# Three matmul split kernel: activation tensors of five stages begin at other addresses modulo 512 bytes

## The chip, the cores and the metric

One core of a Trainium2 chip runs the program. The metric is the device time of one execution in microseconds (us), taken from several runs. The core has TensorE (PE, matmuls; its weight loads are listed as PEld), VectorE (DVE), ScalarE (ACT), GpSimd (POOL) and a queue engine (SP) that issues the weight transfers. On-chip memory (SBUF) has 128 partitions; an address here is a byte offset within a partition, the same in all 128.

## The reference

Two blocks in a row over 256 tokens of width 1024, in float32. The first: nine modulation vectors from a condition, a gated feed-forward part (width 2816) over latent and context tokens, a mixed layer (short convolution branch, grouped attention with 8 query and 2 key heads, gates, output projection), and a second feed-forward part over latent tokens. The second: an even layer (four mLSTM heads and eight stick-breaking attention heads, one output projection of 2048 rows) and an odd layer (multi-scale pooling with a small mixing matrix for each of four groups, gates, an output projection of 2048 rows). Cut to the matmuls that matter here:

```python
x = x + 0.5 * ml[2] * swiglu(modulate(rms_norm(x, norm1_g), ...), ffn1_w_in, ffn1_w_out)   # latent, and the same for the context
x = x + ml[5] * ((g_conv * (y_conv @ w_bc) + g_attn * (o_attn @ w_ba)) @ w_out)
x = x + 0.5 * ml[8] * swiglu(modulate(rms_norm(x, norm3_g), ...), ffn2_w_in, ffn2_w_out)
x = rms_norm(x, final_g)
x = x + rmsnorm(concat(ya, yb) @ w_out_ab, post_g)                 # even layer
mixed = einsum('bsgc,gce->bsge', pooled, pool_w) * pool_scale       # odd layer
x = x + rmsnorm((mixed * silu(z)) @ w_out_c, post_g)
```

## The kernel before, in words

**How a product is made.** Activations lie transposed, features on partitions and tokens along the row (T = 256 latent tokens; 512 with the context). Every weight matrix is cut into chunks of up to 4 x 128 rows by 256 columns, each one DMA into the ring `W`. ScalarE rounds a chunk into `WH` (float32r), VectorE writes the rest `W - WH` into `WL`, both rings of five slots. Activations are split in the same way into a high and a low tensor. A product is then three matmuls into one PSUM tile for each k-tile of 128 rows and each 128 output columns (lines 1048 to 1050, with the weights stationary and the activations moving), or lines 1054 to 1056 with the activations stationary and the weights moving (for `v`, `ev`, `sv` and `p1`):

```python
pe.matmul(o, h[:, k, c], xh[:, kk, a:b], start=kk == 0, stop=False)
pe.matmul(o, h[:, k, c], xl[:, kk, a:b], start=False, stop=False)
mm = pe.matmul(o, l[:, k, c], xh[:, kk, a:b], start=False, stop=kk == gm.nk - 1)
```

A matmul here has 128 stationary columns (512 bytes of a partition) and 256 or 512 moving columns (1024 or 2048 bytes). While one streams, the weight load of the next is under way.

**What sets the order.** The class `Plan` writes one list of steps before anything is built; each engine's program walks that list and does its own share, with semaphores between. Products ("gemms") are called in the order of the model, and small work (attention, mLSTM, stick-breaking, norms) is laid between their chunks. Nothing in `Plan` depends on addresses.

**Where tensors lie.** `sbuf(...)` takes the next free bytes. The rings and shared tensors come first and stay. Below them each stage has a region of its own in a `with ExitStack()` block, and the blocks reuse the same bytes; a `PAD` tensor, which nothing reads or writes, sets where a block's tensors begin. Every slot, chunk, k-tile and 128-column step is a multiple of 512 bytes, so an operand's address modulo 512 is that of its tensor. The built program has these, modulo 512:

| tensor | moving or stationary in | matmuls | address mod 512 | distance from WH, WL |
|---|---|---|---|---|
| WH, WL | all | | 320 | |
| X1H, X1L | fa1, fb1 (first feed-forward, 512 columns) | | 320 | 0 |
| GH1, GL1 | fx1 (512 columns; its last two tiles in halves of 256) | | 320 | 0 |
| XH, XL (parts of XHB, XLB) | all products of normed x, 256 columns; `k` with 512 | | 0 | 192 |
| YH, YL | mc, res | 384 | 0 | 192 |
| OH, OL | ma | 192 | 0 | 192 |
| GH2, GL2 | fx2 (second feed-forward, out) | 528 | 0 | 192 |
| ZH, ZL | p0 (even layer, out) | 384 | 0 | 192 |
| RH, RL | p1 (odd layer, out; stationary) | 384 | 0 | 192 |
| PH, PL | om (odd layer, mixing) | 192 | 0 | 192 |

"Distance" is (tensor - weights) modulo 512. Where the activations are stationary, moving minus stationary is the other way round, 320 for 192.

The stages in order of time: first feed-forward to 405 us, q, k, v and the attention beside cg, vc, bg to 550, gt and mc (YH) in turn to 612, ga, ma (OH) to 658, res (YH) to 681, second feed-forward with fx2 (GH2) twice to 875, even layer to 1121, p0 (ZH) to 1171, odd layer with om (PH) from 1221 to 1292, and p1 (RH) to 1336.

Of the kernel before, what the change touches and what calls it, by code (L numbers as in the profile page):

```python
# [844 lines left out]
def build_program(nc, w, out):  # L845
    with ExitStack() as ctx:
# [12 lines left out]
        def sbuf(st, name, shape, dt=F32):  # L859
            return st.enter_context(nc.sbuf_tensor(name, shape, dt))  # L860
# [31 lines left out]
            AC1 = sbuf(st, "AC1", [128, 4, 256])  # L892
            JK = sbuf(st, "JK", [128, 4, 256])
        with ExitStack() as st:
            sbuf(st, "PAD3", [128, 64])
            YH, YL = sbuf(st, "YH", [128, 8, T], F32R), sbuf(st, "YL", [128, 8, T], F32R)
            OH, OL = sbuf(st, "OH", [128, 8, T], F32R), sbuf(st, "OL", [128, 8, T], F32R)
            Q = sbuf(st, "Q", [128, 8, T])
            K = sbuf(st, "K", [128, 2, 512])
            VV = sbuf(st, "VV", [128, 4, T])  # L900
            MC = sbuf(st, "MC", [128, 8, T])
            U = sbuf(st, "U", [128, 2, T + 2])
            PT = sbuf(st, "PT", [128, 2, 4, T])
            SM = sbuf(st, "SM", [128, 4, 4])
        HOT = MC[:, 0, 0:131]
        with ExitStack() as st:
            sbuf(st, "PAD5", [128, 64])
            GH[2], GL[2] = sbuf(st, "GH2", [128, 12, T], F32R), sbuf(st, "GL2", [128, 12, T], F32R)
        with ExitStack() as st:
            sbuf(st, "PAD6", [128, 64])  # L910
            ZH, ZL = sbuf(st, "ZH", [128, 16, T], F32R), sbuf(st, "ZL", [128, 16, T], F32R)
            G = sbuf(st, "G", [128, 6, T])
            AT = sbuf(st, "AT", [128, 2, 4])
            CV = sbuf(st, "CV", [128, 4, T + 3])
            E = {n: sbuf(st, f"E{n}", [128, 2, 2, T]) for n in "qkvoz"}
            EW = sbuf(st, "EW", [128, 2, 384])
        with ExitStack() as st:
            sbuf(st, "PAD7", [128, 64])
            RH, RL = sbuf(st, "RH", [128, 16, T], F32R), sbuf(st, "RL", [128, 16, T], F32R)
            PH, PL = sbuf(st, "PH", [128, 2, 4, T], F32R), sbuf(st, "PL", [128, 2, 4, T], F32R)  # L920
            OZ = sbuf(st, "OZ", [128, 2, 4, T])
            PV = sbuf(st, "PV", [128, 6, 16 + T])
# [1378 lines left out]
```

## Time and profile before

| | |
|---|---|
| median of 3 runs | 1337.68 us |
| lowest, highest | 1337.42, 1344.29 us |
| profiled execution: span from first to last instruction | 1343.2 us |
| profiled execution: its own time outside the span | not given by the page |
| TensorE busy | 1312.1 us, 9320 matmul records |
| VectorE, ScalarE, GpSimd busy | 903.8, 645.0, 27.3 us |
| read from HBM | 227.63 MB, 170 GB/s over the span |

The profile lists each instruction with its start and a duration; for matmuls the ends are modelled and they overlap, so a matmul's duration (276 to 284 ns at 256 columns) is more than twice the time from one start to the next. That time between starts is what adds up to the span. "Idle before" is an engine's idle time ahead of a group and what ended it. A busy share of TensorE close to 1 means that it never ran dry, not that its matmuls followed at the highest rate.

### The profile page before, as it was taken

The page shows a single profiled execution, that of the slowest core. Times are in us where ns is not written, and L with a number is a line of the kernel's source. Part 1 is how long each engine was busy: PE and PEld are TensorE (multiplying, and loading weights), DVE is VectorE, ACT ScalarE, POOL GpSimd, SP SyncE. Part 2 cuts the span into 40 slices and gives each one's busy share as a digit, 9 for nine tenths or more (in the row PEclk, how much of TensorE's full clock was granted, in tenths as well). Part 3 has the DMA queues.
Part 4 walks back from the last instruction along what each step waited for, and adds up shares of the span by engine and source line. Part 5 has one row for each costly group of instructions (what it writes and reads, how often), then busy time and mean ns, then how long its engine had stood idle before and what let it go on. Part 6 is the DMA issues. An engine that isn't in the chain of part 4 may idle for free. (4 is left out here: it accounts for less than half of the span.)

```text
span 1343.2 us, 23450 instructions
## 1 busy us (share of the span) xinstructions
PE 1312.1 (98%) x9320; PEld 1214.2 (90%) x9320; DVE 903.8 (67%) x1461; ACT 645.0 (48%) x1026; POOL 27.3 (2%) x27
## 2 busy tenths in 40 slices
PE   5999999999999999999999999999999999999998
PEld 3688888888889999999999999998999999999998
DVE  3577875556558497755775555678887666689873
ACT  4432222222336335545554445566666766556553
POOL 0000000000020000000000000200000000100000
PEclk6999999999999999999999999999999999999999
DMA  8746556464554345444545655565556445536660
GB/s 304 262 161 200 190 188 217 160 233 163 190 178 142 111 137 162 137 147 135 180 145 186 199 172 171 164 188 154 155 149 188 142 141 185 162 110 205 207 202 32
DMA packets 201484, 230.20 MB, mean 171 GB/s; under 512 B 7072, under 2 KB 191648, under 8 KB 201376
## 3 DMA queue, kind: packets, MB, share of 16 engines
q1 hardware_dynamic: 201088, 228.42, 53.8%
q8 instruction: 75, 1.23, 0.4%
q10 hardware_dynamic: 288, 0.28, 0.1%
q14 instruction: 33, 0.27, 0.1%
HBM read 227.63 MB, written 1.05 MB: 170 GB/s over the span
## 5 line engine op out<-in xcount | busy, mean ns | idle before, releaser
L1048 PE MATMUL P<-XHB,WH 128*128 128x256 f32 (+1 forms) x1808 | 556.0, 308 | 7.6 <-DVE XLB L1707 3.7
L1049 PE MATMUL P<-XLB,WH 128*128 128x256 f32 (+1 forms) x1808 | 546.0, 302 | 0.0
L1050 PE MATMUL P<-XHB,WL 128*128 128x256 f32 (+1 forms) x1808 | 545.9, 302 | 0.0
L1911 DVE TENSOR_TENSOR WL<-W,WH 128x1024 fp32r<-128x1024 f32 x358 | 431.9, 1225 | 89.9 <-ACT WH L1490 89.7
L1490 ACT ACTIVATE WH<-W 128x1024 fp32r<-128x1024 f32 x358 | 368.8, 1041 | 251.2 <-PE P L1050 162.3
L1048 PEld LDWEIGHTS P<-XHB,WH 128*128 128x128 f32 x1808 | 340.9, 189 | 28.1 <-issue 7.3
L1050 PEld LDWEIGHTS P<-XHB,WL 128*128 128x128 f32 x1808 | 342.2, 189 | 14.8
L1049 PEld LDWEIGHTS P<-XLB,WH 128*128 128x128 f32 x1808 | 340.6, 188 | 15.3 <-issue 0.5
L1048 PE MATMUL P<-GH,WH 128*128 128x256 f32 (+1 forms) x372 | 122.1, 328 | 0.0
L1049 PE MATMUL P<-GL,WH 128*128 128x256 f32 (+1 forms) x372 | 121.5, 327 | 0.0
L1050 PE MATMUL P<-GH,WL 128*128 128x256 f32 (+1 forms) x372 | 121.5, 327 | 0.0
L1781 DVE TENSOR_TENSOR TS<-TS,P 128x512 f32<-128x512 f32 (+1 forms) x44 | 24.3, 554 | 83.2 <-PE P L1050 83.2
L1050 PEld LDWEIGHTS P<-GH,WL 128*128 128x128 f32 x372 | 70.8, 190 | 6.1
L1049 PEld LDWEIGHTS P<-GL,WH 128*128 128x128 f32 x372 | 70.0, 188 | 6.4 <-issue 0.2
L1048 PEld LDWEIGHTS P<-GH,WH 128*128 128x128 f32 x372 | 70.0, 188 | 6.3 <-issue 0.2
L1978 DVE CUSTOM_DVE_ANT_0 W<-W,AC,V 128x1024 f32<-128x1024 f32 x56 | 71.6, 1278 | 0.0
L1351 ACT ACTIVATE GH<-TS 128x512 fp32r<-128x512 f32 (+1 forms) x44 | 23.1, 525 | 92.8 <-DVE TS L1781 92.8
L1345 ACT ACTIVATE TS<-P 128x512 f32<-128x512 f32 (+1 forms) x44 | 21.4, 491 | 86.5 <-PE P L1050 86.5
L1791 DVE SCALAR_TENSOR_TENSOR X<-P,GM,X 128x256 f32<-128x256 f32 x48 | 21.4, 480 | 53.4 <-PE P L1050 53.3
L1054 PE MATMUL P<-WH,XHB 128*128 128x256 f32 x160 | 45.7, 286 | 1.1 <-DVE WL L1911 1.0
L1055 PE MATMUL P<-WL,XHB 128*128 128x256 f32 x160 | 44.6, 279 | 0.0
L1056 PE MATMUL P<-WH,XLB 128*128 128x256 f32 x160 | 44.6, 279 | 0.0
(314 smaller groups left out, 1791.4 us busy)
## 6 DMA issues: line engine op xcount, KB each, us to landing
W<-in_ffn_w_in SPq DMA_DIRECT2D x88, 512.0 KB, 4.8
W<-in_w_in_ab SPq DMA_DIRECT2D x72, 512.0 KB, 4.7
W<-in_w_modt SPq DMA_DIRECT2D x56, 512.0 KB, 3.8
W<-in_w_in SPq DMA_DIRECT2D x52, 512.0 KB, 3.7
W<-in_ffn_w_out SPq DMA_DIRECT2D x40, 512.0 KB, 4.6
W<-in_w_in_c SPq DMA_DIRECT2D x32, 512.0 KB, 4.4
W<-in_w_mod SPq DMA_DIRECT2D x16, 512.0 KB, 7.4
W<-in_w_out_ab SPq DMA_DIRECT2D x16, 512.0 KB, 4.3
```

The source lines that it names most:

```text
L1048: pe.matmul(o, h[:, k, c], xh[:, kk, a:b], start=kk == 0, stop=False)
L1049: pe.matmul(o, h[:, k, c], xl[:, kk, a:b], start=False, stop=False)
L1050: mm = pe.matmul(o, l[:, k, c], xh[:, kk, a:b], start=False, stop=kk == gm.nk - 1)
L1054: pe.matmul(o, xh[:, kk, c], h[:, k, :], start=kk == 0, stop=False)
L1055: pe.matmul(o, xh[:, kk, c], l[:, k, :], start=False, stop=False)
L1056: mm = pe.matmul(o, xl[:, kk, c], h[:, k, :], start=False, stop=kk == gm.nk - 1)
L1345: act.activation(TS[:, f % NS, 0:n], ps, ACT.Silu).then_inc(S["sil" + kind[2]], 1)
L1351: act.activation(GH[m][:, f % 12, :], TS[:, f % NS, 0:n], ACT.Copy).then_inc(S[f"hh{m}"], 1)
L1490: act.activation(h, a, ACT.Copy).then_inc(S["wh"], 1)
L1781: dve.tensor_tensor(TS[:, f % NS, 0:n], TS[:, f % NS, 0:n], ps, ALU.mult).then_inc(S[f"hm{m}"], 1)
L1911: dve.tensor_tensor(l, a, h.bitcast(F32), ALU.subtract).then_inc(S["wl"], 1)
L1978: td = dve.tensor_tensor_reduce(a if v == s.c - 1 else JK[:, :, :], a, (AC0, AC1)[v][:, :, :], 1.0, vec("bmod", 8 * g + k), ALU.mult, ALU. ...
```

## The change

Six tensors' addresses move, in five regions; pads are made longer or shorter and two are added. Everything that lies behind a pad in its region moves with it. The instructions of every engine, their order, shapes and waits are the same as before.

```diff
         with ExitStack() as st:
-            sbuf(st, "PAD3", [128, 64])
+            sbuf(st, "PAD3", [128, 96])
             YH, YL = sbuf(st, "YH", [128, 8, T], F32R), sbuf(st, "YL", [128, 8, T], F32R)
+            sbuf(st, "PAD4", [128, 16])
             OH, OL = sbuf(st, "OH", [128, 8, T], F32R), sbuf(st, "OL", [128, 8, T], F32R)
...
         with ExitStack() as st:
-            sbuf(st, "PAD5", [128, 64])
+            sbuf(st, "PAD5", [128, 32])
             GH[2], GL[2] = sbuf(st, "GH2", [128, 12, T], F32R), sbuf(st, "GL2", [128, 12, T], F32R)
         with ExitStack() as st:
-            sbuf(st, "PAD6", [128, 64])
+            sbuf(st, "PAD6", [128, 80])
             ZH, ZL = sbuf(st, "ZH", [128, 16, T], F32R), sbuf(st, "ZL", [128, 16, T], F32R)
...
         with ExitStack() as st:
-            sbuf(st, "PAD7", [128, 64])
+            sbuf(st, "PAD7", [128, 48])
             RH, RL = sbuf(st, "RH", [128, 16, T], F32R), sbuf(st, "RL", [128, 16, T], F32R)
+            sbuf(st, "PAD8", [128, 64])
             PH, PL = sbuf(st, "PH", [128, 2, 4, T], F32R), sbuf(st, "PL", [128, 2, 4, T], F32R)
```

A pad's unit is 4 bytes. The new addresses modulo 512, from the built program:

| tensor | before | after | distance from WH, WL after |
|---|---|---|---|
| YH, YL | 0 | 128 | 320 |
| OH, OL, and Q, K, VV, MC, U behind them | 0 | 192 | 384 |
| GH2, GL2 | 0 | 384 | 64 |
| ZH, ZL | 0 | 64 | 256 |
| G, AT, CV, E, EW behind ZL | 0, 0, 32, 96, 96 | 64, 64, 96, 160, 160 | |
| RH, RL | 0 | 448 | 128 |
| PH, PL, and OZ, PV behind them | 0 | 192 | 384 |
| all others | | the same | XH 192, X1H and GH1 0 |

## Rows read from the trace of the kernel before

**Rows 1.** The page: busy time of the engines, and TensorE's clock by slices.
```profile
PE 1312.1 (98%) x9320; PEld 1214.2 (90%) x9320; DVE 903.8 (67%) x1461; ACT 645.0 (48%) x1026; POOL 27.3 (2%) x27
...
PEclk6999999999999999999999999999999999999999
```

**Rows 2.** Waits of TensorE: who waited for whom, us in total, times, longest.
```profile
PE P L1083 <- DVE SQ L1932: 8.1, 2, 4.4
PE P L1048 <- DVE XLB L1707: 3.7, 3, 1.4
```

**Rows 3.** Busy us of each engine in each stretch, (x) the instructions.
```profile
core 0: us, PE busy (x) PEld busy (x) DVE busy (x) ACT busy (x) POOL busy (x), PEclk, DMA share, GB/s
180.00:220.00 40.00, 40.00 (x178) 33.16 (x177) 28.12 (x44) 8.00 (x8) 0.00 (x0) 1.00 0.68 223
626.00:881.00 255.00, 253.35 (x2107) 250.27 (x2105) 154.36 (x208) 128.86 (x192) 13.13 (x11) 1.00 0.57 175
700.00:740.00 40.00, 40.00 (x342) 40.00 (x341) 22.90 (x28) 20.57 (x30) 0.00 (x0) 1.00 0.62 191
757.00:781.00 24.00, 24.00 (x206) 24.00 (x205) 12.97 (x17) 8.98 (x9) 0.00 (x0) 1.00 0.65 191
1266.00:1284.00 18.00, 18.00 (x161) 18.00 (x160) 16.54 (x39) 9.39 (x16) 0.00 (x0) 1.00 0.59 193
1294.00:1334.00 40.00, 40.00 (x355) 40.00 (x354) 18.10 (x21) 16.43 (x27) 0.00 (x0) 1.00 0.26 80
```

**Rows 4.** Timeline of TensorE, halves of the first feed-forward part: first and last.
```profile
390.91 0.28 PE L1049 MATMUL P<-GL,WH 128*128 128x256 f32 x1
...
396.79 0.28 PE L1050 MATMUL P<-GH,WL 128*128 128x256 f32 x1
```

**Rows 5.** Timeline of TensorE, the k projection: first and last.
```profile
438.77 0.39 PE L1050 MATMUL P<-XHB,WL 128*128 128x512 f32 x1
...
446.01 0.39 PE L1048 MATMUL P<-XHB,WH 128*128 128x512 f32 x1
```

**Rows 6.** Timeline of TensorE around the last transposes of the attention.
```profile
625.73 0.28 PE L1050 MATMUL P<-XHB,WL 128*128 128x256 f32 x1
...
626.07 0.28 PE L1050 MATMUL P<-XHB,WL 128*128 128x256 f32 x1
626.18 0.60 PE L1164 MATMUL P<-C,TS 128*128 128x128 f32 x4
...
626.74 0.28 PE L1049 MATMUL P<-XLB,WH 128*128 128x256 f32 x1
...
627.45 0.28 PE L1049 MATMUL P<-XLB,WH 128*128 128x256 f32 x1
```

**Rows 7.** Groups of TensorE by form: count | busy us, mean ns; last two of 555:565 and 391:401 us.
```profile
L1049 PE MATMUL P<-GL,WH 128*128 128x256 f32 x216 | 60.8, 281 | 0.0
...
L1049 PE MATMUL P<-YL,WH 128*128 128x256 f32 x128 | 35.7, 279 | 0.0
...
L1049 PE MATMUL P<-ZL,WH 128*128 128x256 f32 x128 | 35.6, 278 | 0.0
...
L1056 PE MATMUL P<-WH,RL 128*128 128x256 f32 x128 | 35.4, 276 | 0.0
...
L1049 PE MATMUL P<-OL,WH 128*128 128x256 f32 x64 | 18.0, 281 | 0.0
...
L1049 PE MATMUL P<-PL,WH 128*128 128x256 f32 x64 | 17.7, 276 | 0.0
...
L1049 PE MATMUL P<-YL,WH 128*128 128x256 f32 x10 | 2.8, 276 | 0.0
...
L1049 PE MATMUL P<-GL,WH 128*128 128x256 f32 x26 | 7.4, 283 | 0.0
```

**Rows 8.** Groups of VectorE by form: the subtraction for GL at both widths.
```profile
L1885 DVE TENSOR_TENSOR GL<-TS,GH 128x512 fp32r<-128x512 f32 x22 | 15.1, 689 | 1.1
...
L1885 DVE TENSOR_TENSOR GL<-TS,GH 128x256 fp32r<-128x256 f32 x22 | 9.3, 422 | 1.6 <-ACT GH L1351 0.3
```

## The prediction

> **What bounds the kernel now.** I read the page first: TensorE is busy for 1312.1 of 1343.2 us and its clock is granted in full in all slices but the first; VectorE stands at 67% and ScalarE at 48% [rows 1]. The list of waits comes next: the longest waits of TensorE for another engine are 8.1 us in all, in the opening, and a few of 1 to 4 us [rows 2]. So the time is the number of matmuls times the distance in time between two starts (the spacing), and a change that moves no instruction can reach the time only through that spacing. The change moves none: instructions, their order, their sizes and their waits stay, and only start addresses differ.
>
> The spacing is not one number. I take it from stretches of the windows view; a count there includes the matmuls cut by the edges, so the spacing is (length + one duration) / count, and where that is too coarse I take first and last start of the timeline. By width and by the distance between moving and stationary operand modulo 512 bytes (the section on the kernel has the addresses):
>
> - 256 columns, distance 192 or 320: (40.28)/355 = 113.5 ns over w_out_c, and (18.28)/161 = 113.5 ns in the om/op/oz stage; but (40.28)/342 = 117.8 and (24.28)/206 = 117.9 ns between 700 and 781 us [rows 3]. Two levels at the same distance. I call them fast and slow.
> - 256 columns, distance 0 (the halves of the first feed-forward part, where GH1 is read 256 wide): 49 spacings between 390.91 and 396.79 us, 120.0 ns [rows 4].
> - 512 columns: distance 0 (40.39)/178 = 226.9 ns [rows 3]; distance 192 (the k projection) 31 spacings between 438.77 and 446.01 us, 233.5 ns [rows 5].
>
> So the distance acts, in both directions: at 256 columns distance 0 is 2.2 to 6.5 ns worse than 192, at 512 columns 6.6 ns better. Fast and slow at one distance look like a state that is kept: up to 626 us the starts are 0.113 us apart (three spacings from 625.73 to 626.07), four transposes come in between, and afterwards they are 0.118 apart (six from 626.74 to 627.45) [rows 6]; that level then lasts for 250 us. The mean duration that the profile gives a matmul follows the level (276 fast, 281 slow, 283 at distance 0), so the groups by form tell what each stage has today: RL and PL 276 (all fast), OL 281 and GL 281 (all slow), ZL 278 (about 60% fast), YL 279 (both: 276 in a window inside mc, so mc is fast and res slow) [rows 7].
>
> **The change part by part.** Counts are from [rows 7], three matmuls per row's count. YH/YL 384, OH/OL 192, ZH/ZL 384, RH/RL 384, PH/PL 192, and GH2/GL2 (216 - 40) x 3 = 528, since 10 k-tiles x 2 tiles x 2 halves = 40 of the GH rows are the halves. Together 2064 matmuls, 9320 are in the program. One step from fast to slow is 4.3 ns, from slow to 120.0 ns 2.2 ns, from fast to 120.0 ns 6.5 ns.
>
> Bounds. All six tensors fast: 192 (res) + 192 (O) + 528 (G) + 154 (40% of Z) = 1066 matmuls gain 4.3 ns, -4.6 us. All six at the level of distance 0: 998 fast ones lose 6.5 ns and 1066 slow ones 2.2 ns, +8.8 us. No row shows distances 64, 128, 256 or 384, so these two are the ends, with one further step (6.6 ns, the difference that the 512-wide rows show between two distances) for what a new distance may add on top.
>
> Term by term, each new distance by the measured distance that is nearest to it on the circle of 512, with d and 512 - d taken as alike because 192 (weights stationary) and 320 (weights moving, as in RH) have the same fast level of 113.5 ns:
> - YH/YL, 320 in place of 192: 320 is measured, same two levels. 0.
> - ZH/ZL, 256: nearest is 192 or 320. 0.
> - GH2/GL2, 64: as near to 0 as 64, and 128 from 192. I take 120.0: 528 x 2.2 = +1.2 us. Bounds -2.3 (fast) and +4.6 (a further step).
> - OH/OL and PH/PL at 384, RH/RL at 128 from the weights (so moving minus stationary 384): 64 from 320, 128 from 0. I take the two levels, drawn anew. R and P are all fast today, O is all slow; at even odds 576 x 0.5 x 4.3 = +1.2 us and 192 x 0.5 x 4.3 = -0.4 us.
>
> Sum: +2.0 us, 1345.2 us of span for an execution like the profiled one. Its span of 1343.2 is 5.5 us over the median of the three runs (1337.68) and near the highest (1344.29); 5.5 us are some 1280 matmuls at the one level and not the other, so part of the runs' spread may be the draw itself. The same +2.0 on the median gives **1339.7 us**.
>
> What the change costs at nothing. Q, K, VV, MC, U, PT, the E tiles, EW, CV, OZ and PV move with the pads and are read by VectorE, ScalarE and plain f32 matmuls. VectorE's subtraction for GL takes 689 ns at 512 elements with all operands at one place modulo 512, and 422 ns at 256 with GH2 192 away from TS [rows 8]: per element (689 - 422)/256 = 1.04 ns, and with that slope 422 - 267 = 155 ns of fixed part for both, so its distance shows no price. The cover is that TensorE waits for it hardly anywhere [rows 2]. If an operation there did grow by, say, 50 ns, the 16 to 48 of a group would cost 1 to 2 us only where TensorE stands waiting.
>
> **The rivals.**
> *B, slower: the new distances pay what distance 0 pays.* Mechanism: the two streams of TensorE, moving and next stationary, disturb each other if they start close to each other modulo 512, and "close" reaches to 128 and 256. The place is p1 and om above all, since these are all fast now: 576 x 6.5 = 3.7 us; Z 154 x 2.2 + 230 x 6.5 = 1.8; G 1.2; O 0.4; sum +7.1, 1344.8 us. With a further step for G alone 1348.3, for all 1680 (without YH) 1355.9. For it: the only other 256-wide distance in the trace is worse than both levels [rows 4]. Against: at 512 columns it is 192 that is worse [rows 5], so nearness is not the whole rule. It decides the sign as soon as 128 and 384 are on its side.
> *C, faster: the draw falls on fast and stays.* All from 626 to 881 us, 2107 matmuls [rows 3], is slow now. If 384 in OH or 320 in res leads to the fast level, and the level is kept over the second feed-forward part as the slow one is now, 2107 x 4.3 = 9.1 us go: 1328.6. For it: levels last [rows 3, 6]. Against: TensorE is interrupted by plain matmuls before that part, and there a new draw is made at distance 192, as before.
> *D, nothing: distance is not what acts.* The levels would be chosen by history alone, and 120.0 ns be a property of that stage; then the time stays 1337.7. Against it stand the 512-wide rows, where one kind of matmul has two spacings at two distances [rows 3, 5]. The Trainium skill (TensorE: Matmul & The Clock Gate, "Part 2: What happens when you issue a matmul") gives such a rule: moving and stationary operand have independent read ports, and loading the next weights "doesn't steal SBUF read bandwidth from the running matmul". By that rule the sum would be 0 in place of +2.0; the trace's 120.0 against 113.5 ns speaks against it.
>
> **How the numbers follow.** My forecast 0.43, B 0.31, C 0.12, D 0.14. A measurement of this kernel can tell about 0.5%, 6.7 us, from no change: below 1331.0 is faster, above 1344.4 slower. Faster: C 0.11 and a lucky draw in the forecast 0.02, 0.13. Slower: B 0.25 (its smaller part stays under the bound) and an unlucky draw 0.05, 0.30. The rest, 0.57, is the same. The range that leaves out 2 in 10 reaches into C at 1331.5 and through B with a further step for G to 1349.
>
> **What the profile after would show.** Right: the same counts, the clock full, no new wait of TensorE; GH2's matmuls at 283 ns and a spacing of 120.0 in its windows; ZL, YL, OL, PL and RL at 276 or 281, XHB stages mixed as before. B: PL and RL at 283 or more, spacing 120 or above in the last 43 us. C: 276 throughout 690 to 880 us. D: GL at 276 or 281. The forecast is wrong if a level that no row has appears (over 120 or under 113 ns), or if XHB stages, which the change doesn't touch, change more than the stages that it does.

## The result and the profile after

| | before | change |
|---|---|---|
| first comparison, median (lowest to highest, runs) | 1337.88 us (1337.42 to 1344.29, 4) | 1349.22 us (1347.77 to 1350.19, 4) |
| repeated later (e12) | 1344.11 us (1337.58 to 1344.89, 15) | 1346.19 us (1344.12 to 1350.80, 11) |
| ratio, first | | 1.0069 [1.0043, 1.0095] |
| ratio, repeated | | 1.0039 [1.0021, 1.0058] |
| span of the profiled executions | 1343.2; later 1340.0 us | 1344.8; later 1342.3 us |

Slower both times, by some 0.5%. The two ratios differ because neither kernel's time is one number: of 82 runs of it in the comparisons of this study 34 lie around 1337.6 us, 44 around 1344.0 and 4 around 1349.6, with a mean of 1341.6; the 15 runs of the change have a mean of 1347.8, 6.2 us or 0.46% more, 9 of them from 1344.1 to 1348.5 us and 6 from 1349.9 to 1350.8. The first four runs of before were mostly low ones.

The page of the change shows, as [rows 1], a TensorE that is never short of work, at the same clock:

```profile
PE 1313.2 (98%) x9320; PEld 1215.2 (90%) x9320; DVE 904.5 (67%) x1461; ACT 645.4 (48%) x1026; POOL 27.0 (2%) x27
...
PEclk6999999999999999999999999999999999999999
```

The waits of TensorE, as [rows 2], are the same two within 0.4 us (lines stand two further down, for the two new pads ahead of them):

```profile
PE P L1085 <- DVE SQ L1934: 7.7, 2, 4.4
PE P L1050 <- DVE XLB L1709: 3.7, 3, 1.3
```

So it is the spacing above all that can have changed. The windows view of the change; the columns are those of [rows 3], and the number to read is the count behind PE:

```profile
180.00:220.00 40.00, 40.00 (x178) 33.14 (x177) 28.36 (x46) 7.53 (x8) 0.00 (x0) 1.00 0.68 221
640.00:656.00 16.00, 16.00 (x136) 16.00 (x135) 12.31 (x23) 7.83 (x12) 0.00 (x0) 1.00 0.54 163
690.00:870.00 180.00, 180.00 (x1566) 179.82 (x1565) 109.90 (x141) 94.59 (x137) 7.28 (x5) 1.00 0.59 182
700.00:740.00 40.00, 40.00 (x355) 40.00 (x355) 24.18 (x31) 21.04 (x30) 0.00 (x0) 1.00 0.66 205
757.00:781.00 24.00, 24.00 (x206) 24.00 (x206) 12.86 (x16) 9.56 (x9) 0.00 (x0) 1.00 0.64 198
1142.00:1163.00 21.00, 21.00 (x177) 21.00 (x176) 13.89 (x18) 12.82 (x20) 4.70 (x5) 1.00 0.59 180
1264.00:1280.00 16.00, 16.00 (x139) 16.00 (x138) 14.17 (x33) 8.33 (x14) 0.00 (x0) 1.00 0.60 195
1294.00:1334.00 40.00, 40.00 (x339) 40.00 (x338) 17.36 (x19) 15.59 (x26) 0.00 (x0) 1.00 0.24 74
```

The same view of a second profiled execution of the kernel before (run e4 below):

```profile
640.00:656.00 16.00, 16.00 (x138) 16.00 (x138) 14.09 (x25) 8.55 (x12) 0.00 (x0) 1.00 0.48 139
690.00:870.00 180.00, 180.00 (x1582) 179.44 (x1581) 110.86 (x142) 95.43 (x142) 7.27 (x5) 1.00 0.61 186
757.00:781.00 24.00, 24.00 (x214) 24.00 (x214) 12.81 (x16) 9.56 (x9) 0.00 (x0) 1.00 0.67 202
1294.00:1334.00 40.00, 40.00 (x343) 40.00 (x342) 15.36 (x20) 15.11 (x29) 0.00 (x0) 1.00 0.15 50
```

By (length + one duration) / count:

- w_out_c (RH, 1294 to 1334) went from 113.5 to (40.28)/339 = 118.8 ns. But in the second execution of before it took (40.28)/343 = 117.4 ns (the window's last 1.2 us hold the closing plain matmuls there). The same program has two levels here.
- GH2 (757 to 781) stands at 117.9 ns in the change. In [rows 3] it was 117.9 as well, in the second execution of before (24.28)/214 = 113.5.
- 690 to 870 us, all of the second feed-forward part: 1528 matmuls in the first execution of before (118.0 ns), 1582 in the second (114.0), 1566 in the change (115.1). Against the one the change wins (1566 - 1528) x 0.116 = 4.4 us, against the other it loses 1.8 us. XHB, which the change doesn't touch, is at 113.5 ns there (700 to 740), where [rows 3] had 117.8; in the second execution of before it is at 113.5 too.

The groups of TensorE by form, as [rows 7], show the stages one by one, with the caution that a mean duration of 281 covers spacings from 117.8 to 118.9:

```profile
L1051 PE MATMUL P<-GL,WH 128*128 128x256 f32 x216 | 60.6, 281 | 0.0
L1051 PE MATMUL P<-ZL,WH 128*128 128x256 f32 x128 | 36.2, 283 | 0.0
...
L1058 PE MATMUL P<-WH,RL 128*128 128x256 f32 x128 | 36.0, 281 | 0.0
...
L1051 PE MATMUL P<-YL,WH 128*128 128x256 f32 x128 | 35.8, 279 | 0.0
...
L1051 PE MATMUL P<-OL,WH 128*128 128x256 f32 x64 | 18.2, 284 | 0.0
...
L1051 PE MATMUL P<-PL,WH 128*128 128x256 f32 x64 | 18.0, 282 | 0.0
```

Finer than a window is the mean over every uninterrupted step from one start to the next, stage by stage, from the trace. These are the numbers that I use from here on (ns, 256 columns; behind @ the distance from the weights):

| | matmuls | before, 1st | before, 2nd (e4) | change | change, 2nd (e12) |
|---|---|---|---|---|---|
| YH | 384 | 115.63 @192 | 115.64 | 117.77 @320 | 117.77 |
| OH | 192 | 117.78 @192 | 117.78 | 120.03 @384 | 120.03 |
| GH2 | 528 | 117.78 @192 | 113.37 | 117.78 @64 | 117.78 |
| ZH | 384 | 115.15 @192 | 115.15 | 119.90 @256 | 119.90 |
| PH | 192 | 113.33 @192 | 117.80 | 118.89 @384 | 118.73 |
| RH, stationary | 384 | 113.34 @192 | 117.79 | 118.65 @128 | 118.65 |
| XHB, moving | 4344 | 115.87 @192 | 115.25 | 114.70 @192 | 114.29 |
| XHB, stationary | 480 | 117.11 @192 | 117.35 | 116.89 @192 | 117.56 |

Each tensor at a new distance has nearly the same spacing in both executions of the change; PH alone differs, by 0.16 ns. What is at 192 moves between 113.3 and 117.8, in GH2, PH and RH as a whole. YH, OH and ZH are at 192 as well and show the same mean both times, so two executions show no draw there.

Most of PH's 0.16 ns comes from one stretch: in the first profile of the change its first 24 matmuls settle at another level than the later ones:

```profile
1219.25 0.28 PE L1050 MATMUL P<-PH,WH 128*128 128x256 f32 x1
...
1221.65 0.28 PE L1052 MATMUL P<-PH,WL 128*128 128x256 f32 x1
```

That is 2.40/20 = 120.0 ns, where the next stretch (20 steps from 1227.59 to 1229.96) has 118.5. So distance 384 has 120.0 in one stretch and 118.5 to 118.9 in the others. The XHB stretch ahead of the one with 120.0 ran at 117.8; but two more with 117.8 ahead of them have 118.7 and 118.8, so that is not the whole reason.

**The account.** Against the second execution of before: YH 384 x 2.13 = 0.82, OH 0.43, GH2 528 x 4.41 = 2.33, ZH 384 x 4.75 = 1.82, PH 0.21, RH 0.33, together +5.9 us; XHB gives back 4344 x 0.55 + 480 x 0.46 = 2.6; sum +3.3, where the spans differ by 4.8 (1.5 us lie in none of these rows, which leave out every step of over 150 ns, the pauses). Against the first: 0.82 + 0.43 + 0 + 1.82 + 1.07 + 2.04 = +6.2, XHB -5.2, sum +1.0, where the spans differ by 1.6.

### The profile page after: what moved, and what is told of

Same layout as the page of the kernel before. It is cut to its first block and busy times, and to the rows that moved or that the text cites. A ratio compares the mean times of both kernels' runs of the same rounds, so it can differ in the third digit from the quotient of the medians.

```text
span 1344.8 us, 23450 instructions
## 1 busy us (share of the span) xinstructions
PE 1313.2 (98%) x9320; PEld 1215.2 (90%) x9320; DVE 904.5 (67%) x1461; ACT 645.4 (48%) x1026; POOL 27.0 (2%) x27
```

## The experiments

Three questions: is it the distance that acts, and with what rule; which of the six moves costs; and what sets the level at distance 192. A tensor's bytes are rounded up to 32, so every address is a multiple of 32.

**e4: before again.** No edit.

> The kernel before, unchanged, for a second profile. If fast and slow at distance 192 are drawn in each execution, the XHB and GH2 matmuls are fast in other stretches than in the first profile (its share of fast ones was 44% for XHB, 0 for GH2), and the span moves by several us with that share, 4.4 ns for each matmul. If they are set by the program, the same stretches are slow again, 626 to 881 us above all.

Measured: 1342.50 us, rows above. The two levels are no property of the program: GH2 was slow and then fast, PH and RH fast and then slow. The second feed-forward part, GH2 and the XHB about it, is worth (1582 - 1528) x 0.116 = 6.3 us, PH and RH 576 x 4.45 = 2.6 us and more with the XHB between them. Two draws of this size fit the three clusters of before's times; that each cluster is one combination of them is my reading, since only two executions of it have a profile.

**e1 and e2: half of the change each.** e1 has the edits from PAD6 down (ZH @256, RH @128, PH @384), e2 those of PAD3 to PAD5 (YH @320, OH @384, GH2 @64).

```diff
 e1                                          e2
-PAD6 [128, 64]   +PAD6 [128, 80]           -PAD3 [128, 64]   +PAD3 [128, 96]
-PAD7 [128, 64]   +PAD7 [128, 48]                             +PAD4 [128, 16]
                  +PAD8 [128, 64]           -PAD5 [128, 64]   +PAD5 [128, 32]
```

> Only the last two regions of the change: ZH/ZL at 256, RH/RL at 128, PH/PL at 384; YH, OH and GH2 stay at 192. Theory 1 (the distance of a stage sets the spacing of its matmuls): ZH 120.0 ns, RH 118.6, PH about 118.9, all others as before, so most of the change's loss is here: 384 x 4.8 + 384 x 5.3 + 192 x 5.6 ns = 4.9 us of it, time near 1343 to 1345 us if the kept level of the XHB matmuls is drawn as before. Rival (the loss of 11 us comes with the XHB matmuls' level, drawn anew after a moved stage): ZH, RH and PH show what they show, but the whole 11 us do not split; this kernel would be at 1338 or at 1349 and its XHB matmuls on one level over hundreds of us.

> Only the first two regions of the change: YH/YL at 320, OH/OL at 384, GH2/GL2 at 64; ZH, RH and PH stay at 192. Theory 1: YH 117.8 ns, OH 120.0, GH2 117.8 at all times, RH and PH back at 113.3; against the profile of before +0.8 and +0.4 us, and up to 528 x 4.4 = 2.3 us more where before had GH2 on the fast level: 1338.5 to 1341.5 us. Rival: as for the other half, 1338 or 1349.

Measured, against 1342.20 us of before in the same job (1336.49 to 1349.67, 23 runs): e1 1343.86 (1341.27 to 1350.65, 12), ratio 1.0030 [1.0006, 1.0054]; e2 1344.10 (1340.31 to 1347.65, 12), ratio 1.0017 [0.9995, 1.0039]. Windows of e1, and then of e2:

```profile
757.00:781.00 24.00, 24.00 (x214) 24.00 (x214) 13.67 (x16) 9.08 (x10) 0.00 (x0) 1.00 0.64 198
1142.00:1163.00 21.00, 21.00 (x176) 20.99 (x175) 11.96 (x15) 11.19 (x15) 2.75 (x3) 1.00 0.65 196
1294.00:1334.00 40.00, 40.00 (x340) 40.00 (x339) 14.88 (x19) 15.35 (x29) 0.00 (x0) 1.00 0.16 52
```

```profile
690.00:870.00 180.00, 180.00 (x1561) 179.34 (x1560) 109.88 (x139) 93.85 (x136) 7.28 (x5) 1.00 0.59 182
757.00:781.00 24.00, 24.00 (x206) 24.00 (x206) 12.86 (x16) 8.81 (x9) 0.00 (x0) 1.00 0.65 197
```

ZH costs its 119.9 ns and RH its 118.65 in e1, GH2 its 117.8 in e2, as in the whole change: the moves act one by one. By their ratios the halves cost 0.30 and 0.17%, together 0.47%, which lies between the two measurements of the whole, 0.39 and 0.69%. The time of e2 was expected at 1338.5 to 1341.5 us and came out at 1344.10: the expectation added 1.2 to 3.5 us to a time of before near 1337.5, its low cluster, and the runs of e2 spread as well (1340.31 to 1347.65). The rival of a time at 1338 or 1349 with nothing between is out for both.

**e3: the distances dealt out anew among the stages.** YH @448, OH @128, GH2 @128, ZH @448, RH @256, PH @64: PAD3 and PAD6 gone, a pad of 48 ahead of OH, PAD5 48, PAD7 80, one of 80 ahead of PH.

> Every moved tensor at a distance it had in neither kernel: YH 448, OH 128, GH2 128, ZH 448, RH 256, PH 64; XHB stays at 192. Theory 1 (spacing follows distance, not stage): PH at 64 shows 117.8 ns as GH2 did at 64, RH at 256 shows 120.0 as ZH did at 256, YH and ZH (both 448) agree with each other, OH and GH2 (both 128) agree with each other. Rival (each stage has a spacing of its own, or what counts is which side is stationary): PH and RH stay at 118.6 to 118.9 or return to 113.3, and the pairs differ.

Measured: 1343.37 us. YH 113.53, ZH 115.15, OH 120.03, GH2 118.68, PH 117.79, RH 119.98 ns. So 64 is 117.8 whether GH2 or PH has it, 256 is 120 whether ZH (moving) or RH (stationary) has it, and YH and ZH @448 show levels that 192 has shown, YH 113.53 in both its stages.

**e5 and e6: steps of 32 bytes, and distances at 512 columns.** e5 has GH1 @64 (PAD2 32), e6 GH1 @128 (PAD2 48) and XHB @448 (XH at 112 in XHB). The other pads ask for distances between these; by the rounding, 144 landed at 160, 176 at 192, 208 at 224 and 240 at 256, so the rival of e5, about odd multiples of 16, had no test.

> Distances that are no multiple of 64: YH 160, OH 176, GH2 208, ZH 224, RH 240, PH 144; the first feed-forward part's GH1 (512 columns) at 64 in place of 0; XHB stays at 192. The spacings found so far repeat every 256 bytes: 0 and 256 120.0 ns, 64 and 320 117.8, 128 and 384 118.6 to 120.0, 192 and 448 either 113.3 or 117.8. Theory 1 with period 256: 144 to 176 lie between 118.6 to 120.0 and the two levels, 208 to 240 between the two levels and 120.0, and none is under 113.3; GH1 at 64 has another spacing than 226.7 ns, 220.0 or 233.3, one step of 6.7 ns away. Rival (what counts is the 64-byte or 32-byte line in which an operand starts, not a distance): the odd multiples of 16 (144, 176, 208, 240) differ from 160 and 224 by more than from each other.

> XH/XL at 448 in place of 192 (4824 matmuls), with YH 32, OH 96, GH2 240, ZH 208, RH 160, PH 224, and GH1 at 128. Theory 1 with period 256: XHB shows the same two levels of 113.3 and 117.8 ns as at 192 and the k projection 233.5 ns; the time moves by what the small tensors do, at most some 2 x 4 us, so 1340 to 1350 us. Rival (448 is always fast, as YH at 448 was in the last look, 113.5 ns in gt/mc and in res, where it had been slow in every kernel at 192): XHB at 113.3 throughout, 4344 x 1.5 to 2.5 ns = 6 to 11 us less.

Measured: e5 1345.11 us; e6 1352.12 (1349.70 to 1352.21, 4) against 1338.53 (7), ratio 1.0094 [1.0064, 1.0124]. In e5, YH @160 117.97, OH @192 117.78, GH2 and ZH @224 118.32, PH @160 117.50, RH @256 119.98 ns; in e6, YH @32 116.84, OH @96 120.02, GH2 @256 119.93, ZH @224 118.33, PH @224 118.13, RH @160 120.00 ns. XHB @448 has both levels, 115.35 ns on average (117.8 in the stretch of 539 from 697 us, 113.4 in that of 480 from 795), and the k projection 233.4 at 448 as at 192. So 448 is no always fast place, which was the rival of e6; its time, expected at 1340 to 1350 us, is some 2 us over that. At 512 columns, the timeline of e5 (41 steps) and of e6 (39 steps), first and last:

```profile
371.61 0.39 PE L1050 MATMUL P<-GH,WH 128*128 128x512 f32 x1
...
380.99 0.39 PE L1052 MATMUL P<-GH,WL 128*128 128x512 f32 x1
```

```profile
371.74 0.39 PE L1052 MATMUL P<-GH,WL 128*128 128x512 f32 x1
...
380.84 0.40 PE L1052 MATMUL P<-GH,WL 128*128 128x512 f32 x1
```

9.38/41 = 228.8 ns at distance 64 and 9.10/39 = 233.3 at 128, where distance 0 has 226.7 and 192 has 233.5 [rows 5]; e5 had expected 220.0 or 233.3. No finer place is better than the fast level of 192 at 256 columns, and none better than 0 at 512. The finer places don't line up in one curve: 32 has 116.84, under the slow level of 192, and 160 has 117.50 to 117.97 with the activations moving, while OH @96 and RH @160 have 120.0.

**Which way the distance counts when the activations are stationary** these runs don't settle. 0 and 128 are the same both ways round modulo 256, so RH @256 and @128 can't tell. RH @192 says that it is tensor minus weights: the other way round it would be at 64, where the moving tensors have 117.8 and never 113.3. RH @160 says the opposite: 120.00 as OH has at 96, its place the other way round, and not 117.5 to 118.0 as YH and PH @160. It is the weaker sign, since OH has 120.0 at 128 too.

**e7: weights and activations moved together.** A pad of 192 bytes ahead of WH moves the weights and all that lies behind them, so that their own places change and their distances don't; the other pads keep YH @320, OH @384, ZH @256, RH @128, and give GH2 @128 and PH @64.

```diff
+        sbuf(ctx, "PADW", [128, 48])
```

> WH, WL and all that lies behind them begin 192 bytes later (a pad ahead of WH), so the weights lie at 0 modulo 256 and no more at 64; the distances from the weights are ones already measured: YH 320, OH 384, GH2 128, ZH 256, RH 128, PH 64, XHB 192. Theory 1 (the distance between the two operands counts): 117.8, 120.0, 118.7, 119.9, 118.65, 117.8 ns, XHB with 113.3 and 117.8. Rival (an operand's own place modulo 256 counts, since until now the weights never moved and each distance stood for one place): activations at 64 show 120 (YH, PH), at 128 117.8 (OH, GH2, RH), at 0 113.3 or 117.8 (ZH), and XHB at 192 118.6 to 120.0, some 4 ns more on 4824 matmuls, 19 us more in all.

Measured: 1346.51 us; YH 117.77, OH 120.03, ZH 119.91, RH 118.67, GH2 118.69, PH 117.79 ns: within 0.02 ns of the same distances elsewhere. XHB @192 is at 114.71 moving, and the rival's 19 us are not there. It is the distance between the two operands that counts, not where either lies. The windows of GH2 (24.28/205 = 118.4, one count is 0.6 ns) and RH:

```profile
757.00:781.00 24.00, 24.00 (x205) 24.00 (x204) 12.65 (x15) 9.29 (x9) 0.00 (x0) 1.00 0.65 198
1294.00:1330.00 36.00, 36.00 (x305) 36.00 (x305) 15.96 (x18) 15.16 (x25) 0.00 (x0) 1.00 0.24 75
```

**e9: XH itself at distance 256, everything else as before.**

```diff
-        XHB = sbuf(ctx, "XHB", [128, 4096 + 48], F32R)
-        XLB = sbuf(ctx, "XLB", [128, 4096 + 80], F32R)
+        XHB = sbuf(ctx, "XHB", [128, 4096 + 64], F32R)
+        XLB = sbuf(ctx, "XLB", [128, 4096 + 64], F32R)
```

(with XH at 64 in XHB and X1L at 64 in XLB, for 48 and 80.)

> Only XH/XL move, from 192 to 256 (4344 matmuls with them moving at 256 columns, 480 with them stationary, 48 at 512 columns). Theory 1 with period 256: 120.0 ns at all of them at 256 columns in place of a mean of 114.4 to 115.9 and 117, so 4344 x 4.1 to 5.6 + 480 x 2.8 = 19 to 26 us more, and the k projection at 226.7 ns as at distance 0; the time 1358 to 1366 us. The six tensors keep two levels, though their draws come out otherwise, since the runs of XHB between them have one level only. Rival (spacings differ, but the time lost is that of the draw, which a shift of many tensors only disturbs): some us, no more than the 13 us between the fastest and slowest run of the kernel before.

Measured: 1354.96 us (1354.20 to 1356.00, 7) against 1343.08 (10), ratio 1.0101 [1.0070, 1.0132]. XHB at 119.85 ns, and the k projection at 5.89/26 = 226.5 ns (26 steps from 439.67 us), as at distance 0. YH, OH, GH2, PH and RH, left at 192, now run at 113.71, 113.43, 113.45, 113.93 and 113.34, all fast; ZH keeps its mix, 115.07. No run lies more than 1.8 us from another. The time was expected at 1358 to 1366 us and is 3 us under that. One part of the miss is that the stages left at 192 are fast; another that TensorE pauses less: its steps of over 150 ns inside the XHB stages sum to 22.7 us, where the first execution of before has 27.2. Its windows:

```profile
640.00:656.00 16.00, 16.00 (x143) 16.00 (x143) 11.34 (x19) 8.10 (x11) 0.00 (x0) 1.00 0.53 164
700.00:740.00 40.00, 40.00 (x335) 40.00 (x334) 23.25 (x31) 19.45 (x29) 0.00 (x0) 1.00 0.64 195
757.00:781.00 24.00, 24.00 (x212) 24.00 (x211) 13.88 (x19) 10.23 (x11) 0.00 (x0) 1.00 0.58 182
```

OH (first row, 113.8 ns by the window) was slow in both profiled executions of before. What is new is its neighbour: a stretch at 256 runs just ahead of it. Over the profiles of before, the change, e1 to e3, e4 to e7 and e9, a stretch at 192 that follows one at 0, 32 or 64 (modulo 256) without a pause came out fast 46 times of 46. Behind one at 128 or 224 the first six steps are nearly all slow, 117.5 to 118.8 ns, but most such stretches don't stay so: by their last six steps 15 of 22 are fast, 9 of 15 behind 128 and 6 of 7 behind 224; behind 160 all nine are.

Does that explain what XHB gives back in the change? GH2 @64 lies between the XHB stretches of the second feed-forward part, and they are fast in both its profiles. But the longest of them, 539 matmuls from 693 us, runs before GH2 does, and the one behind GH2 is fast with GH2 at other distances too. The window from 790 to 830 us, all XHB, in the first and second execution of before, the change, e3 (GH2 @128), e5 (@224) and e7 (@128):

```profile
790.00:830.00 40.00, 40.00 (x342) 40.00 (x341) 22.55 (x28) 19.86 (x29) 0.00 (x0) 1.00 0.58 175
790.00:830.00 40.00, 40.00 (x355) 40.00 (x355) 22.05 (x31) 20.71 (x30) 0.00 (x0) 1.00 0.59 184
790.00:830.00 40.00, 40.00 (x356) 40.00 (x355) 22.52 (x27) 20.45 (x29) 0.00 (x0) 1.00 0.60 185
790.00:830.00 40.00, 40.00 (x356) 40.00 (x355) 21.84 (x27) 20.81 (x30) 0.00 (x0) 1.00 0.64 193
790.00:830.00 40.00, 40.00 (x355) 40.00 (x354) 22.31 (x27) 20.64 (x29) 0.00 (x0) 1.00 0.59 185
790.00:830.00 40.00, 40.00 (x355) 40.00 (x354) 22.20 (x27) 20.75 (x29) 0.00 (x0) 1.00 0.60 186
```

Only the first execution of before is slow there, at 40.28/342 = 117.8 ns; all the others have 113.1 to 113.5. So the 4.4 us that came back in this part are mostly that one execution's slow draw, and that the change caused them is not shown.

**e8: one plain f32 matmul of constants ahead of every XHB product**, 154 in all, of 64, 128, 256 or 512 columns in turn, to see which sets the level.

```diff
+                        pe.matmul(ps[:, 0:n], con("one"), C[:, off:off + n], start=True, stop=True)
```

> The kernel before, with one plain f32 matmul of constants ahead of each XHB product of 256 columns (some 90 of them, in eight kinds: 64, 128, 256 or 512 columns, moving operand at 192 or 0 modulo 256), its output overwritten by the product that follows. It asks what draws the level at distance 192. Theory: the level is set by where the streams stand to each other when the matmuls start again after something else, and then kept; in the eight profiles at hand 512-column score matmuls are followed by fast 110 times in 112, rope's by slow 43 times in 45. Then each of the eight kinds has its own outcome, nearly always the same. Rival (chance in each execution): fast and slow after every kind. Either way 90 x 0.2 to 0.9 us more, 1375 to 1390 us.

Measured: 1376.32 us, (1376.32 - 1343.08)/154 = 0.22 us for each. By the six steps behind each of those that stand alone, the level was slow 14 times of 15 after 512 columns, 13 of 16 after 256, but fast 13 of 15 after 128 and 10 of 18 after 64. The width of what comes before has a say, though 64, 128 and 256 columns each have both outcomes, so neither theory holds as it stands. The scores of the attention, plain matmuls of 512 columns too, seem to say the opposite, "fast 110 times in 112"; but the matmul that stands last before the product is mostly another. The timeline of before at both kinds of place:

```profile
506.00 1.02 PE L1159 MATMUL P<-K,Q 128*128 128x512 f32 x2
...
506.97 0.28 PE L1049 MATMUL P<-XLB,WH 128*128 128x256 f32 x1
...
507.91 0.28 PE L1048 MATMUL P<-XHB,WH 128*128 128x256 f32 x1
```

```profile
513.23 0.59 PE L1159 MATMUL P<-K,Q 128*128 128x512 f32 x1
513.65 0.60 PE L1164 MATMUL P<-C,TS 128*128 128x128 f32 x4
...
514.22 0.28 PE L1049 MATMUL P<-XLB,WH 128*128 128x256 f32 x1
...
514.90 0.28 PE L1049 MATMUL P<-XLB,WH 128*128 128x256 f32 x1
```

Directly behind the scores, once in each profile, XHB @192 is slow (0.94/8 = 117.5 ns here, and in all twelve profiles that have it @192); behind scores and then four transposes of 128 columns it is fast (0.68/6 = 113.3 here, and 64 times of 64 in before, the change, e1 to e5 and e7). That is what the single matmuls of 512 and of 128 columns showed. It is still no rule: the transposes at 626 us are followed by slow in every one of these profiles [rows 6].

**e10 and e11: one extra matmul of the kind of line 1048 (float32r activations against WH) at ten places**, ahead of XHB products of ga, fb2, oz and op, at distance 0 (e10) or 128 (e11). Its result is overwritten, so the output stays.

```diff
+                    if kk == 0 and j == 0 and (kind, gm.g, gm.i) in KICKED:
+                        pe.matmul(ps[:, 0:256], h[:, k, 0:128], xh[:, kk, a - 48:b - 48], start=True, stop=True)
```

(16 for 48 in e11.)

> The kernel before with ten extra split-type matmuls, each the first of a product of XHB (ga 3; fb2 0, 4, 12; five products op and oz of the odd layer's groups 1 to 3 and one more), its moving operand read 192 bytes earlier, at distance 0; its output is overwritten. In the eleven profiles so far, wherever a stretch at distance 0, 32 or 64 is followed without a pause by one at 192, the one at 192 is fast (46 of 46), while after 128 or 224 it is mostly slow. Theory (the last matmul before draws the level, and it is then kept): OH, res, the whole second feed-forward part, om and p1 are at 113.3 ns in every execution; cost 10 x 0.12 = 1.2 us, gain 2 us at OH and res, and 7 and 5 us in those executions that had the second feed-forward part or the end slow: 1335 to 1338 us and less spread than the 13 us of the kernel before. Rival (a long stretch is needed, or chance): levels as before, 1 us slower.

> The same ten extra matmuls, the moving operand 64 bytes earlier, at distance 128. Theory (the distance of the last matmul before draws the level): mostly slow after them, so the second feed-forward part and the end are at 117.8 ns more often than in the kernel before: 1342 to 1350 us. Rival (any extra matmul restarts the streams and that alone makes them fast): the same levels and time as with distance 0.

Measured, against 1343.59 us of before in the same job (1336.57 to 1349.72, 23 runs): e10 1338.90 (1338.27 to 1345.09, 12), ratio 0.9982 [0.9961, 1.0004]; e11 1338.90 (1336.69 to 1339.85, 12), ratio 0.9978 [0.9959, 0.9998]. The distance of the extra matmul made no difference to the median, so the theory of e11, 1342 to 1350 us, is out. Under 1340 us lie 9 of the 23 runs of before, 9 of e10's 12 and all 12 of e11's; and 1337.6, the low cluster of before, plus 10 x 0.12 us is 1338.8. So the runs look like the low cluster with the price of ten matmuls on it, drawn more often. Whether the extra matmuls are what makes it so, the two profiles, both of low runs, can't tell. Windows of e11:

```profile
690.00:870.00 180.00, 180.00 (x1581) 179.43 (x1581) 110.95 (x142) 94.83 (x139) 7.27 (x5) 1.00 0.60 184
757.00:781.00 24.00, 24.00 (x214) 24.00 (x214) 13.32 (x16) 9.09 (x10) 0.00 (x0) 1.00 0.64 198
```

1581 and 214 are the counts of the fast draw. But a single extra matmul shows how little is understood. The timeline of e11 around the first (line 1037), in a slow stretch:

```profile
627.56 0.28 PE L1055 MATMUL P<-XHB,WL 128*128 128x256 f32 x1
627.68 0.28 PE L1037 MATMUL P<-XHB,WH 128*128 128x256 f32 x1
627.79 0.28 PE L1053 MATMUL P<-XHB,WH 128*128 128x256 f32 x1
...
628.60 0.28 PE L1054 MATMUL P<-XLB,WH 128*128 128x256 f32 x1
...
629.06 0.28 PE L1055 MATMUL P<-XHB,WL 128*128 128x256 f32 x1
629.17 1.89 PE L1176 MATMUL P<-PT,VV 128*128 128x256 f32 x8
```

Up to some 0.7 us behind it the steps are still 0.118, then 0.114 (628.60 to 629.06 in four), and the plain matmuls at 629.17 draw anew (OH is slow again). In e10 the same place stays slow throughout. The other nine stood in stretches that were fast already: the steps about each rise to 115 to 122 ns in e11 and 118 to 124 in e10, for four steps, and are 113 again behind them. In these two profiles, then, no extra matmul turned the second feed-forward part or the end from slow to fast; they were fast when it came. OH stays at 117.8 in both, where the theory of e10 had 113.3. e11 is the one version whose interval lies under 1, with a median 4.7 us under before's in the same job and a spread of 3 us in place of 13. The interval only just excludes no change, the mechanism is open, and I would not ship it without more runs.

**e12: the change again.** Its times stand in the first table, as the repeat.

> The changed kernel, unchanged, in five rounds: so far it has four times (1347.8 to 1350.2 us), while the kernel before, over 70 runs, spreads from 1336.1 to 1349.7 with a mean of 1341.3, so its first four, with a median of 1337.9, were on the low side. Theory (the six tensors' spacings cost 4 to 6 us, other distances give XHB back 2 to 4 us of it, the rest is the draw): median 1344 to 1349, 4 to 7 us over the kernel before and not 11; the six tensors at the same spacings as in the first profile to 0.2 ns, since these are no draw. Rival (the 11 us are real and something beside the matmuls' spacing is lost): the ratio stays at 1.0069 or above.

Measured: 1346.19 us, ratio 1.0039 [1.0021, 1.0058]; every stage within 0.2 ns of its first profile but XHB, 114.29 for 114.70 moving and 117.56 for 116.89 stationary. The interval lies under 1.0069, so the rival that the first 11 us are real is out.

## Why the prediction was right or wrong

The forecast was 1339.7 us, "the same" likeliest at 0.57, range 1331.5 to 1349.0. The change is slower by 0.4 to 0.7%, about the bound of what can be told from no change; its median was 1349.22 in the first comparison, 0.2 over my range, and 1346.19 in the second.

- *What bounds the kernel.* Right. Busy time, clock and waits are the same; most of the difference is in the spacing (3.3 of 4.8 us against the second execution of before, 1.0 of 1.6 against the first), and distance acts on it.
- *Two levels at one distance, "a state that is kept".* Right, and more than I made of it. I took the levels of one execution as those of the program. e4 has GH2 fast and PH and RH slow, the reverse of [rows 7], so "R and P are all fast today" was one draw. I had worked out that the span stood 5.5 us over the median, "some 1280 matmuls at the one level", and then still set my forecast on the median of three runs; their mean over many runs is 1341.6, 3.9 us higher. Of the 8.1 us between the forecast and the change's mean of 1347.8 this is nearly half. That the median of the repeat, and not that of the first comparison, lies in the range is luck with such draws.
- *YH @320, "same two levels. 0."* Mis-sized: 117.77 in both profiles, +0.8 us. The step that failed is "d and 512 - d taken as alike". I took 320 from RH, where it was moving minus stationary; measured as tensor minus weights, RH was at 192 like the rest, and with the activations moving 320 had never been measured. 192 and 320 are not alike there: YH has 115.6 at the one and 117.8 at the other. Which way to count for RH stays open (e5 and e6).
- *ZH @256, "nearest is 192 or 320. 0."* Failed: 119.90, +1.8 us. The rule repeats every 256 bytes, so 256 is 0: the level of distance 0 was in [rows 4]. e3, e6 and e7 confirm it (119.98, 119.93, 119.91).
- *GH2 @64, 120.0 ns, +1.2 us.* The size failed: 117.78 in all. Against the first execution of before that is 0, against the second +2.3 us.
- *OH, PH @384 and RH @128, "the two levels, drawn anew", +0.8 us.* This is the step that failed most plainly. None of them shows the two levels of 192: they have 120.03, 118.7 to 118.9 and 118.65 ns in the profiles of the change. Against the first execution of before +3.5 us (0.43 + 1.07 + 2.04), against the second +1.0. That OH has 120.0 where GH2, PH and RH have 118.7 to 118.9 at the same distance modulo 256 I can't explain; OH always follows an XHB stretch at 117.8, GH2 in e3 and e7 one at 113.3, and PH has had 120.0 once, behind one at 117.8.
- *Sum.* +2.0 forecast for these; measured +6.2 or +5.9. XHB, which I had left at nothing, differs by -5.2 or -2.6, but it is at 192 and drawn anew in each execution; the part of the change in that is not shown.
- *Rival B*, that the new distances pay, had the right sign: 7.1 us by its price of 120.0 for all, 6.2 us of difference between the means. Its mechanism, nearness that reaches to 128 and 256, was half right: no new distance has the fast level, but the order by distance is 120.0 at 0, 117.8 at 64, 118.7 or 120.0 at 128, 113.3 or 117.8 at 192, so 128 is worse than 64.
- *Rival C*, the fast draw over 626 to 881 us, happened in part and not through the change, as far as the runs show: XHB is fast there, as in the second execution of before, but GH2 is not, so 4.4 us came back and not 9.1, and only against a slow draw of before. Its mechanism, 384 in OH leading to the fast level, failed: OH is at 120.0 and res behind it at 117.8.
- *Rival D*, no effect, is refuted: one matmul form has 113.3 to 120.0 ns by distance alone (e1, e3, e7). The rule of the Trainium skill (TensorE: Matmul & The Clock Gate, "Part 2: What happens when you issue a matmul") is that loading the next weights takes nothing from the running matmul's reads. If it is the load that disturbs, 113.3 against 120.0 ns speaks against that rule; no run here took the load away to show that it is.
- *What would prove it wrong.* "If XHB stages change more than the stages that it does": that came close in the first comparison of profiles, -5.2 against +6.2 us. The other sign, a level over 120 or under 113 ns, did not come: OH's 120.03 is the level of distance 0. But 118.7, between the known levels, was a level that no row had, and the sign as I wrote it passes over that.

What stays open: what makes the level at distance 192, why XHB and GH2 share it, why OH at 128 modulo 256 differs, and which way the distance counts with stationary activations. Not tried: addresses finer than 32 bytes, the high and low tensors at different distances, bfloat16.

## What to carry to other kernels

When TensorE is full and only its spacing is left, read the spacing from starts, stage by stage, and profile the kernel before twice: a stage that differs between two executions of one program is a draw, and its level is no evidence on an edit. Nor is a neighbour's: look for an execution of the kernel before that shows the same. Compare operand addresses as a difference modulo 256 bytes; here the fast level of 192 was never beaten for 256 float32r columns, but its slow level was (116.8 at 32), and 0 not for 512. When times come in clusters, the median of three runs is a draw too; the means over ten or more settle half a per cent.

## What the runs showed of the hardware that I had not expected

- TensorE's spacing depends on the distance between the two operands' addresses modulo 256 bytes (e3, e5 to e7, e9), at the full granted clock: at 256 columns 119.9 to 120.0 ns at 0, 117.8 at 64, 118.7 to 120.0 at 128, and at 192 either 113.3 or 117.8. At 512 columns it is 226.7 at 0, 229.0 at 64, 233.3 at 128 and 233.5 at 192: the order is another.
- At 192 there are two levels, kept over hundreds of matmuls, and one program takes the one or the other from execution to execution: 6.3 us in the second feed-forward part of a 1340 us kernel. At 128 one stretch of PH had 120.0 ns and the others 118.5 to 118.9.
- What ran just before has a say in the level at 192: fast 46 times of 46 behind a stretch at 0, 32 or 64; slow 14 times of 15 behind a single plain matmul of 512 constant columns, and fast 13 of 15 behind one of 128. It is not all: most stretches behind 128 or 224 begin slow and end fast (15 of 22).
